# PEER expert table: the gate product joins the one-hot comparison on VectorE, one operation per token

## What is computed

```python
idx, gate = peer_route(hf, lw['peer_w_q'], lw['peer_sub_keys'])   # idx = ia * 128 + ib
act = gelu(einsum('td,thkd->thk', hi, eu[ii]))
y   = einsum('thk,thkd->td', act * gi, ev[ii])
```

## Time and profile before

| what | value |
|---|---|
| median of three runs | 3403.08 us |
| profiled execution: span between first and last instruction | 3393.9 us |
| TensorE busy, share of the span | 92% |
| VectorE busy | 58% |
| ScalarE busy | 38% |
| GpSimd busy | 6% |

### The profile page before, as it was taken

One profiled execution on the slowest core, in us unless ns is written; L12 is line 12 of the kernel. 1 busy time (PEld: TensorE's weight loads), 2 busy tenths in 40 slices (PEclk: granted clock), 3 DMA queues, 4 the chain that ended last, 5 costly groups with the idle time before them and its releaser, 6 DMA issues.

```text
span 3393.9 us, 63208 instructions
## 1 busy us (share of the span) xinstructions
PE 3112.1 (92%) x23603; PEld 2921.9 (86%) x23603; DVE 1973.4 (58%) x3888; ACT 1291.3 (38%) x2225; POOL 190.1 (6%) x203
## 2 busy tenths in 40 slices
PE   6999899799999998922899999999889999999989
PEld 6999689499755787922799999999889999999979
DVE  4477466422233235488766666666766666666654
ACT  4455320122222024411544444444444444444444
POOL 0000110000000000002400000000330000000000
PEclk8999899599999999966999999999999999999989
DMA  5555200356576444400155455455225554545543
GB/s 192 177 184 180 85 1 8 127 199 245 200 250 214 185 160 148 173 0 0 70 180 184 177 182 182 177 185 175 73 99 176 184 179 180 184 175 185 178 148 125
DMA packets 82022, 519.76 MB, mean 153 GB/s; under 512 B 9186, under 2 KB 9458, under 8 KB 28914
## 3 DMA queue, kind: packets, MB, share of 16 engines
q1 hardware_dynamic: 69394, 468.36, 38.8%
q0 software_dynamic: 11360, 45.61, 3.7%
q10 hardware_dynamic: 1152, 4.19, 0.3%
HBM read 508.74 MB, written 9.39 MB: 153 GB/s over the span
## 4 chain that ended last, share of the span: by engine, by line
PE 88%; DVE 7%; POOL 2%; SPq 2%; issue 1%; ACT 0%; DMA 0%; POOLq 0%; DVEq 0%; ACTq 0%
PE ps L551 23%; PE ps L552 23%; PE ps L553 22%; PE ps L915 3%; PE ps L858 3%; PE ps L869 3%; PE ps L978 2%; POOL arena L1335 2%; PE ps L732 1%; SPq L465 1%; PE ps L611 1%; DVE arena L1865 1%; PE ps L546 1%; PE ps L720 1%; PE ps L603 1%
## 5 line engine op out<-in xcount | busy, mean ns | idle before, releaser
L551 PE MATMUL ps<-split 128*128 128x264 f32 x6288 | 1798.0, 286 | 53.9 <-DVE split L393 53.9
L552 PE MATMUL ps<-split 128*128 128x264 f32 x6288 | 1789.7, 285 | 0.0
L553 PE MATMUL ps<-split 128*128 128x264 f32 x6288 | 1784.7, 284 | 0.0
L393 DVE TENSOR_TENSOR split<-arena,split 128x512 fp32r<-128x512 f32 x1568 | 1078.6, 691 | 956.9 <-ACT split L388 954.1
L388 ACT ACTIVATE split<-arena 128x512 fp32r<-128x512 f32 x1568 | 987.8, 632 | 1401.5 <-PE ps L553 1401.1
L551 PEld LDWEIGHTS ps<-split 128*128 128x128 f32 x6288 | 1187.9, 189 | 73.9 <-issue 36.2
L552 PEld LDWEIGHTS ps<-split 128*128 128x128 f32 x6288 | 1188.3, 189 | 0.8
L553 PEld LDWEIGHTS ps<-split 128*128 128x128 f32 x6288 | 1183.6, 188 | 0.3
L1910 DVE TENSOR_TENSOR arena<-arena,ps 128x264 f32<-128x264 f32 x512 | 216.4, 423 | 5.9 <-PE ps L553 5.9
L1335 POOL TENSOR_TENSOR arena<-arena 128x512 f32<-128x512 f32 x66 | 121.7, 1844 | 1264.6 <-DVE arena L1865 1264.6
L978 PE MATMUL ps<-arena 128*128 128x128 f32 x1056 | 140.3, 287 | 38.9 <-POOL arena L1335 38.8
(11 more groups left out here) (299 smaller groups left out, 1696.4 us busy)
## 6 DMA issues: line engine op xcount, KB each, us to landing
arena<-in_wd SPq DMA_DIRECT2D x280, 1024.0 KB, 4.8
arena<-in_vd SPq DMA_DIRECT2D x128, 1024.0 KB, 4.8
arena<-in_kx POOLq DMA_DIRECT2D x32, 512.0 KB, 6.4
arena<-in_kx SPq DMA_DIRECT2D x32, 512.0 KB, 4.5
arena<-in_vx SPq DMA_DIRECT2D x32, 512.0 KB, 4.3
arena<-in_vx POOLq DMA_DIRECT2D x32, 512.0 KB, 4.4
arena<-in_state POOLq DMA_DIRECT2D x8, 512.0 KB, 6.7
o_ss<-arena ACTq DMA_DIRECT2D x8, 512.0 KB, 7.5
```

Of the source, the lines that this page charges most:

```text
L393: nc.vector.tensor_tensor(ckl(q), at(WR + (s % 4) * D_MODEL + q * QW, QW), as_f32(ckh(q)), ALU.subtract).then_inc(lo_ready, 1)
L551: mm(out, wh, xh, start=start, stop=False)
L552: mm(out, wh, xl, start=False, stop=False)
L553: return mm(out, wl, xh, start=False, stop=stop)
```

## The change

On VectorE, the comparison of 8 tokens in one instruction is replaced by 8 instructions, one for each token. Each compares the 64 numbers with the token's `ia`, a per-partition scalar, and multiplies the outcome by the token's gate, a second per-partition scalar. The eighth adds one to `oha_ready`. The comparison for `OHB` is the same as before. The loop over iterations is written out as 33 groups with constant addresses and constant wait counts. On GpSimd the multiplication and its loop are removed, and with them the semaphore `oh_step`. TensorE and ScalarE are not changed.

```diff
-            for half in range(2):
-                def gate_rows(it, j):
-                    pool.wait_ge(oh_step, it * 4 + (33 * half + j + 1))
-                    oh = at(OHA + (j % 2) * 8 * HALF, 8 * HALF).rearrange("p (t a) -> p t a", a=HALF)
-                    gate = arena[:, bass.ds(it * 32 + (IDX + 2 * T + 8 * j), 8)].unsqueeze(2).broadcast_to([P, 8, HALF])
-                    nc.gpsimd.tensor_tensor(oh, oh, gate, ALU.mult).then_inc(oha_ready, 1)
-
-                with pool.Fori(0, 8) as it:
-                    for j in range(4):
-                        gate_rows(it, j)
-                gate_rows(8, 0)
-
...
-                def onehot_a(it, j, lead):
-
-                    if not lead:
-                        dve.wait_ge(pe_job, it * 8 + (PJ[wb + 2 * j] - 3))
-                    oh = at(OHA + (j % 2) * 8 * HALF, 8 * HALF).rearrange("p (t a) -> p t a", a=HALF)
-                    ia = arena[:, bass.ds(it * 32 + (IDX + 8 * j), 8)].unsqueeze(2).broadcast_to([P, 8, HALF])
-                    V.tensor_tensor(oh, cst(C_IOTA + half * HALF, HALF).unsqueeze(1).broadcast_to([P, 8, HALF]), ia,
-                                    ALU.is_equal).then_inc(oh_step, 1)
-
-                    V.tensor_tensor(at(OHB + (j % 2) * 8 * P, 8 * P).rearrange("p (t b) -> p t b", b=P),
+                def onehots(g):
+
+                    if g >= 2:
+                        dve.wait_ge(pe_job, PJ[wb + 2 * g - 3])
+                    for t in range(8):
+                        c = IDX + 8 * g + t
+                        ins = V.tensor_scalar(at(OHA + (g % 2) * 8 * HALF + t * HALF, HALF), cst(C_IOTA + half * HALF, HALF),
+                                              at(c, 1), at(c + 2 * T, 1), ALU.is_equal, ALU.mult)
+                    ins.then_inc(oha_ready, 1)
+                    V.tensor_tensor(at(OHB + (g % 2) * 8 * P, 8 * P).rearrange("p (t b) -> p t b", b=P),
                                     cst(C_IOTA).unsqueeze(1).broadcast_to([P, 8, P]),
-                                    arena[:, bass.ds(it * 32 + (IDX + T + 8 * j), 8)].unsqueeze(2).broadcast_to([P, 8, P]),
+                                    at(IDX + T + 8 * g, 8).unsqueeze(2).broadcast_to([P, 8, P]),
                                     ALU.is_equal).then_inc(ohb_ready, 1)
...
-                for j in range(4):
-                    onehot_a(0, j, j < 2)
-                with dve.Fori(1, 8) as it:
-                    for j in range(4):
-                        onehot_a(it, j, False)
-                onehot_a(8, 0, False)
+                for g in range(33):
+                    onehots(g)
```

More of the change, by code:

```diff
@@ L332, in build @@
         eg_ready, convs_ready = sem("eg_ready"), sem("convs_ready")
-        mg_step, oh_step = sem("merge_step"), sem("onehot_step")
+        mg_step = sem("merge_step")
         def wait_done(eng, n):
```

## The result

The changed kernel took 3422.88 us, the median of four runs (3414.86 to 3424.37), against 3403.15 us for the kernel before (four runs, three of them those of the median given ahead): a ratio of 1.0063, with a 95% interval of 1.0046 to 1.0080. It is slower, by some 20 us; 3428.5 had been forecast, with 3394 to 3434 as range. A later session, with six runs of the changed kernel beside ten of the kernel before, gave 1.0048 (1.0035 to 1.0061).

The account below looks back on a forecast made before the run. A ring of waits was taken to bound the kernel before, VectorE's load after. 42.1 + 256i us at i = 0.234 made each half 12.7 us longer, +25.4 on the median 3403.08: 3428.5 us, range 3394 to 3434.

Parts of the forecast that it names:

- The mechanism: Table stages: GpSimd's steps leave, eight small operations per group make VectorE's own load the pace, 3.00 us per group.
- 8i + 1.13 us per group: VectorE's load in the table stages: eight small operations at i each, start to start, plus 1.13 us for the second comparison.
- The cover of the second comparison: Table stages: L1868, 1.21 us, was hidden beside GpSimd's 1.86 us step; the change puts it on VectorE's path.
- The price i: Start-to-start cost of one small VectorE operation with two per-partition scalars: between 0.171 and 0.234 us, 0.234 taken.
- The sum: Length of one table stage (a half): 42.1 + 256i us, giving 102.0 us, 12.7 more than before.
- the rule weighed there: VectorE SBUF operation: 58 cycles plus elements by speed-up at 0.96 GHz, nothing for a scalar; 94 ns for 64 elements.
- a ring of waits: Table stages before: VectorE, GpSimd and TensorE in turn, back to the same buffer in 5.16 us, 2.58 us per group.
- the ring that was left: Table stages after: VectorE and TensorE waiting on each other, 8i + 3.51 us for two groups, 4i + 1.76 each.
- The rest outside the span: Whole kernel: reported time lies 9.2 us above the profiled span, so the difference was added to the median of 3403.08.
- free scalars at 0.105 us per operation: Rival for the table stages: scalars cost nothing, 75.9 us a stage, 13.4 less a half, 3376 us in all; chance 0.04.
- a second scalar for nothing: Rival for the small operations: both scalars fetched together, i = 0.171, 85.9 us a stage, 3396.2 in all; chance 0.20.
- The clock: Rival for the table stages: TensorE's clock falls, 3.4 us per group, 24 us more, 3452 in all; chance 0.04.

## Why the prediction was right, and where it was not

**The mechanism** was right for the changed kernel. VectorE became the bound with 8i + 1.13 us per group, no wait of VectorE for TensorE was left in the steady part (three buffers changed nothing in the pace), the written-out loop counted for nothing, and the 747.21 us between the tables stayed to the hundredth.

**The cover of the second comparison** was not there to lose. The prediction took L1868 as hidden beside GpSimd's step and laid bare by the change. It is on the path in the changed kernel (halved, it gave back 0.525 of 0.53 us), but halved beside GpSimd's step it gave back 0.53 us as well. That the time came out near in spite of it is no merit of this step: the sum set the stage as measured before against VectorE's own load after, and the cover stands in neither.

**The price i** decided the sign, and the higher of its two values was nearer: 0.224 us measured, 0.234 taken, 0.1845 the point of no change. The second scalar was put at 0.063 us after the first one's price and ScalarE's row for two; it measured 0.061. What was too high was the operation with one scalar, 0.171 us where one scalar measures 0.1625: I took it down from 128 elements by the slope between two rows, 0.46 ns per element, while the copies of 64 elements, at 0.105 us, with one scalar's 0.06 added, would have given 0.165.

**The sum** of 42.1 + 256i us gives 99.4 us at the measured i, against 99.84 and 99.77. The forecast of +25.4 us against 21.05 in the two stages is thus the term i, 0.01 us too much in 512 operations, 5.1 us, with 0.8 us the other way.

By the rule weighed there, the Trainium skill's "VectorE: DVE Perf Modes", § The TRN2 errata, 64 elements at double rate are an estimated 94 ns. The runs agree with it within 10 ns where no scalar is read (0.104 us) and differ where one or two are (0.163, 0.224): the measurement decides, and a scalar is a term of its own.

**The reading of the kernel before** was wrong in one step, the first. The prediction said that a ring of waits sets the pace, 5.16 us for two groups. The kernel with three buffers has no such ring and keeps the pace. What bound the kernel was GpSimd's step and VectorE's comparisons taking turns; the sign of it was in the earlier trace rows, where the same comparison takes 0.69 us alone and 1.53 beside GpSimd, and in the earlier trace rows, where it takes 0.88. The forecast did not suffer, since GpSimd's removal ended this alternation, and the ring that was left lay under VectorE's load.

**The rest outside the span** was misread as well. The prediction took 9.2 us between span and reported time to lie outside the instructions. In every run that lists both, it is 1.6 to 1.8 us, so the profiled execution of the kernel before will have taken some 3395.6 us (an estimate; its reported time is not on record), less than the median of 3403.08. Since only a difference was added to the median, nothing came of it.

**The rivals** did not come true, but where a run made one's condition true, its time held: free scalars at 0.105 us per operation were put at 75.9 us a stage, and the kernel without scalars took 74.5; a second scalar for nothing at 85.9, and the kernel with one took 84.1. The clock did not fall: the stages, their low start included, were granted 0.95 and 0.97 where it was 0.95 and 0.96 before, with TensorE busy 2.02 of 2.91 us.

## What to carry to other kernels

Price a short VectorE operation from start to start and by its per-partition scalars: here each scalar cost 0.06 us on 64 elements that cost 0.10 us themselves, so an operation per token lost to one more operation for eight tokens. Two operations whose rows overlap need not work at the same time: make one shorter and see whether the other's row shrinks by as much before you call either of them covered. A steady period that equals the sum of a ring is no proof that the ring sets it: give the ring one more buffer and see.

## What the runs showed of the hardware beyond that

VectorE's comparisons, which have two SBUF inputs, and GpSimd's multiplication keep each other out. The rows do not show it as a wait but as length: VectorE's 128 x 512 comparison 0.69 us alone and 1.53 beside GpSimd, GpSimd's 128 x 512 product 1.95 us beside a comparison of 1,024 elements and 1.42 beside one of 512. The Trainium skill, "SBUF — State Buffer", § Who interferes with whom, says that a VectorE instruction with two SBUF inputs contends with a GpSimd instruction that reads SBUF, since its second input comes through a read interface that the two engines share under an exclusive lock. The two runs agree, down to the 0.53 us by which one's length followed the other's. No run here tried a VectorE operation with one SBUF input beside GpSimd.
